# A 256-token, three-layer fp32 network: the third layer's two 16-column gate tiles as one tile with 48 stationary weight columns

## What is computed

```python
def rmsnorm_2(x, w):
    xf = x.astype(jnp.float32)
    xf = xf * lax.rsqrt(jnp.mean(xf * xf, axis=-1, keepdims=True) + EPS)
    return (xf * w.astype(jnp.float32)).astype(x.dtype)
...
    h = rmsnorm_2(x, ln1_w)
    proj = h @ w_in
    z, xbc, dt_raw, q, k, v, f_raw = jnp.split(proj, split_at, axis=-1)
...
    dt = jax.nn.softplus(dt_raw.astype(jnp.float32) + dt_bias.astype(jnp.float32))
...
    log_f = jax.nn.log_sigmoid(f_raw.astype(jnp.float32) + fox_f_bias.astype(jnp.float32))
```

## Time and profile before

| | us |
|---|---|
| median of three runs | 2963.93 (2962.32 to 2968.41) |
| the profiled execution | 2967.45 |
| its span | 2965.5 |
| TensorE matmul busy | 2497.8 (84%) |
| TensorE weight load busy | 1786.3 (60%) |
| VectorE busy | 1626.1 (55%) |
| ScalarE busy | 949.8 (32%) |
| mean granted TensorE clock | 0.97 of 2.4 GHz |

### The profile page before, as it was taken

One profiled execution on the slowest core, in us unless ns is written; L12 is line 12 of the kernel. 1 busy time (PEld: TensorE's weight loads), 2 busy tenths in 40 slices (PEclk: granted clock), 3 DMA queues, 4 the chain that ended last, 5 costly groups with the idle time before them and its releaser, 6 DMA issues.

```text
span 2965.5 us, 31159 instructions
## 1 busy us (share of the span) xinstructions
PE 2497.8 (84%) x12386; PEld 1786.3 (60%) x12386; DVE 1626.1 (55%) x2261; ACT 949.8 (32%) x1555; POOL 694.8 (23%) x751
## 2 busy tenths in 40 slices
PE   7999888999999999999899387777777677777776
PEld 6997877899898799789689332222222232222222
DVE  4757494544445544346556976656555444444444
ACT  4557455533775443343554110000010001000001
POOL 6003150000000000440000243333334343333331
PEclk9999999999999999899899699999999999999999
DMA  6644304555444535244255699999999999999997
GB/s 195 206 143 142 114 1 154 173 185 182 151 151 143 184 122 193 73 133 152 71 185 171 246 404 422 421 422 421 421 422 422 421 421 422 422 421 422 421 422 318
DMA packets 200416, 779.53 MB, mean 263 GB/s; under 512 B 16564, under 2 KB 20880, under 8 KB 134096
## 3 DMA queue, kind: packets, MB, share of 16 engines
q0 software_dynamic: 74400, 537.15, 43.8%
q1 hardware_dynamic: 125872, 240.40, 24.4%
HBM read 775.40 MB, written 2.10 MB: 262 GB/s over the span
## 4 chain that ended last, share of the span: by engine, by line
DMA 34%; PE 27%; DVE 5%; issue 1%; ACT 1%; POOL 0%; DVEq 0%; ACTq 0%; POOLq 0%
DMA VROW<-in_peer_v_dram,WORK 33%; PE bank L1720 26%; DMA UROW<-in_peer_u_dram,WORK 1%; DVE WL L1089 1%; DVE BIG L1680 1%; DVE WORK L1385 0%; DVE BIG L1386 0%; DVE WORK L1388 0%; DVE WORK L1387 0%; PE bank L1774 0%; DVE WORK L1384 0%; PE bank L1817 0%; DVE BIG L1395 0%; DVE WORK L1397 0%; DVE BIG L1393 0%
## 5 line engine op out<-in xcount | busy, mean ns | idle before, releaser
L1720 PE MATMUL bank<-VROW,WORK 128*128 128x512 f32 x2024 | 926.8, 603 | 368.2 <-DMA VROW<-in_peer_v_dram,WORK 301.2
L1720 PEld LDWEIGHTS bank<-VROW,WORK 128*128 128x128 f32 x2024 | 367.3, 190 | 927.0 <-issue 745.7
L1680 DVE CUSTOM_DVE_ANT_0 BIG<-UROW,bank 128x2048 f32<-128x2048 f32 x256 | 585.5, 2288 | 562.7 <-DMA UROW<-in_peer_u_dram,WORK 548.5
L1089 DVE TENSOR_TENSOR WL<-RAW,WH 128x1024 fp32r<-128x1024 f32 (+2 forms) x464 | 544.4, 1182 | 544.2 <-ACT WH L594 542.9
L594 ACT ACTIVATE WH<-RAW 128x1024 fp32r<-128x1024 f32 (+2 forms) x464 | 465.9, 1020 | 480.6 <-PE bank L1720 480.1
L1720 PE MATMUL bank<-HH,WH 128*128 128x256 f32 x2112 | 604.0, 286 | 8.0 <-issue 4.8
L1720 PE MATMUL bank<-HL,WH 128*128 128x256 f32 x2112 | 598.7, 283 | 0.0
L1720 PE MATMUL bank<-HH,WL 128*128 128x256 f32 x2112 | 598.5, 283 | 0.0
L1720 PEld LDWEIGHTS bank<-HH,WH 128*128 128x128 f32 x2112 | 406.2, 192 | 14.3 <-issue 12.2
L1720 PEld LDWEIGHTS bank<-HL,WH 128*128 128x128 f32 x2112 | 406.4, 192 | 0.0
L1720 PEld LDWEIGHTS bank<-HH,WL 128*128 128x128 f32 x2112 | 406.2, 192 | 0.0
(11 more groups left out here) (322 smaller groups left out, 1739.8 us busy)
## 6 DMA issues: line engine op xcount, KB each, us to landing
RAW<-in_w_in_odd_dram SPq DMA_DIRECT2D x64, 1024.0 KB, 5.0
RAW<-in_w_in_even_dram SPq DMA_DIRECT2D x48, 1024.0 KB, 5.0
RAW<-in_w_in_dram SPq DMA_DIRECT2D x44, 1024.0 KB, 4.9
RAW<-in_w_out_even_dram SPq DMA_DIRECT2D x16, 1024.0 KB, 5.0
RAW<-in_w_out_odd_dram SPq DMA_DIRECT2D x16, 1024.0 KB, 5.0
RAW<-in_w_out_dram SPq DMA_DIRECT2D x16, 1024.0 KB, 5.1
RAW<-in_peer_wq_dram SPq DMA_DIRECT2D x16, 1024.0 KB, 5.1
UROW<-in_peer_u_dram,WORK POOLq DMA_INDIRECT x256, 27.0
```

Of the source, the lines that this page charges most:

```text
L1089: dve.tensor_tensor(WL[:, sl:sl + 2, 0:w], raw[:, k0:k0 + 2, 0:w], WH[:, sl:sl + 2, 0:w].bitcast(F32), ALU.subtract).then_inc(s["wl_done"], 1)
L1680: dve.tensor_tensor_reduce(out=JUNK[:, n % 2, :], in0=UROW[:, b, :], in1=TT, op0=ALU.mult, op1=ALU.add, scale=1.0, scalar=0.0, accum_out=D ...
L1720: return pe.matmul(dst, lhsT, rhs, start=start, stop=stop, skip_group_check=True)
```

## The change

Tile 39 becomes one gate tile of 48 weight columns and tile 44 goes; all later tiles move up by one number (57 in all). Of the 48 columns, 32 are columns 2560 to 2591 (`dt_raw` and 16 of `q`, whose results are not used), 16 are `f_raw`. Each of the four pieces is loaded by two DMAs, each with a semaphore of its own, and ScalarE waits for both. The weights are the stationary side now, 256 tokens move: 6 matmuls per sub-step, 48 in all, into 48 partitions of one bank. ScalarE copies them to GATES_T unscaled; at place G_TURN TensorE turns them with two transposes into bank 5, and one place later ScalarE scales them into DTF with four small copies (`gates_out`). VectorE's F_GATE and S_GATE wait for those. S_CONV moves eight places up with the tiles that it follows; F_FIRST and S_GATE keep their place numbers.

```diff
@@ -77,9 +77,9 @@
         ("odd_out", [("w_out_odd", 0, 512, 4, "res", 0)]),
-        ("two_in", [("w_in_2", 2576, 512, 2, "eighth", 5), ("w_in_2", 5648, 16, 1, "gate", 1),
+        ("two_in", [("w_in_2", 2576, 512, 2, "eighth", 5), ("w_in_2", 2560, 48, 1, "gate", 0),
                     ("w_in_2", 3600, 512, 2, "chan", 7), ("w_in_2", 4624, 512, 2, "tok", 9),
-                    ("w_in_2", 2560, 16, 1, "gate", 0), ("w_in_2", 1024, 512, 3, "chan", 2),
+                    ("w_in_2", 1024, 512, 3, "chan", 2),
                     ("w_in_2", 0, 512, 2, "silu", 0)]),
...
@@ -124,10 +124,11 @@
 C_ACT_LAG, C_DVE_LAG = 2, 3
-F_GATE = 8 * TWO_TILE + 30
+G_TURN = 8 * TWO_TILE + 29
+F_GATE = 8 * TWO_TILE + 31
 F_FIRST = 8 * TWO_TILE + 47
 S_GATE = 8 * TWO_TILE + 70
-S_CONV = 8 * TWO_TILE + 86
+S_CONV = 8 * TWO_TILE + 78
 Q_TILE = last_tile("two_out") + 1
...
@@ -242,7 +243,7 @@
             const_in vec_in masks vec_t cols_set x_in lnf_in out_done eps_set act_chain dve_chain pool_chain
-            w_full0 w_full1 w_full2 w_full3 wh_done wl_done ws_used tile_free
+            w_full0 w_full1 w_full2 w_full3 w_gate0 w_gate1 w_gate2 w_gate3 g_t wh_done wl_done ws_used tile_free
             n_rstd n_sq n_sum n_x n_t n_xt n_h n_l r_diag r_row r_set t_scaled y_ready y_h y_l
...
@@ -294,6 +295,7 @@
                               two_slots(WORK[:, 2304:3072]))
+        GATES_T = WORK[0:48, 3200:3456]
         C_T, C_SP, C_W = (two_slots(WORK[:, 0:768]), two_slots(WORK[:, 768:1536]), two_slots(WORK[:, 1536:2304]))
@@ -338,7 +340,12 @@
                     c = bass.ds(r["c0"] + i * r["width"], r["width"])
-                    sp.dma_start(dst, src[:, 4 * j:4 * j + 4, c]).then_inc(s[f"w_full{j}"], 16)
+                    if r["kind"] == "gate":
+                        sp.dma_start(dst[:, :, 0:32], src[:, 4 * j:4 * j + 4, 2560:2592]).then_inc(s[f"w_gate{j}"], 16)
+                        sp.dma_start(dst[:, :, 32:48], src[:, 4 * j:4 * j + 4, 5648:5664]).then_inc(s[f"w_full{j}"], 16)
+                    else:
+                        sp.dma_start(dst, src[:, 4 * j:4 * j + 4, c]).then_inc(s[f"w_full{j}"], 16)
...
@@ -558,19 +565,29 @@
                 act.wait_ge(s["ws_used"], 8 * (t + 1))
+                if kind == "gate":
+                    act.activation(GATES_T, bank[2 * parity][0:48, 0:T], ACT.Copy).then_inc(s["tile_free"], 1)
+                    return
                 if kind != "plain":
...
                     rstd = SM[:, 20 + b:21 + b]
-                    if kind == "gate":
-                        ins = act.activation(DTF[:, r["dest"], b, :], ps[:, 0:16], ACT.Copy, scale=rstd)
-                    else:
-                        w = r["width"]
-                        ins = act.activation(BIG[:, r["dest"] + i, b * 512:b * 512 + w], ps[:, 0:w], ACT.Copy,
-                                             scale=rstd if kind == "tok" else 1.0)
+                    w = r["width"]
+                    ins = act.activation(BIG[:, r["dest"] + i, b * 512:b * 512 + w], ps[:, 0:w], ACT.Copy,
+                                         scale=rstd if kind == "tok" else 1.0)
                 ins.then_inc(s["tile_free"], 1)
+            def gates_out():
+                act.wait_ge(s["g_t"], 1)
+                act.wait_ge(s["n_rstd"], NORMED.index("two_in") + 1)
+                for b in range(2):
+                    for d in range(2):
+                        ins = act.activation(DTF[:, d, b, :], bank[5][:, 64 * b + 32 * d:64 * b + 32 * d + 16], ACT.Copy,
+                                             scale=SM[:, 20 + b:21 + b])
+                ins.then_inc(s["g_t"], 1)
...
@@ -585,6 +602,8 @@
                         act.wait_ge(s[f"w_full{sub // 2}"], 16 * (t + 1))
+                        if r["kind"] == "gate":
+                            act.wait_ge(s[f"w_gate{sub // 2}"], 16)
                     if r["base"] > 0 or not first or sub >= 4:
@@ -842,6 +861,8 @@
                     attend_step("f_", i, F_S, F_PROBS, F_PT, None)
+                if place == G_TURN + 1:
+                    gates_out()
                 if place == F_GATE + 2:
...
@@ -1466,7 +1487,7 @@
                 if place == F_GATE:
-                    dve.wait_ge(s["tile_free"], TWO_TILE + 3)
+                    dve.wait_ge(s["g_t"], 2)
                     link(dve.tensor_tensor(f_lf.rearrange(two, m=2), DTF[:, 1, :, :], per_head(F_FB), ALU.add))
...
@@ -1474,7 +1495,7 @@
                 if place == S_GATE:
-                    dve.wait_ge(s["tile_free"], TWO_TILE + 8)
+                    dve.wait_ge(s["g_t"], 2)
                     dve.tensor_tensor(s_dt.rearrange(two, m=2), DTF[:, 0, :, :], per_head(S_DTB), ALU.add)\
...
@@ -1486,7 +1507,7 @@
-                    dve.wait_ge(s["tile_free"], TWO_TILE + 9 + k // 4)
+                    dve.wait_ge(s["tile_free"], TWO_TILE + 8 + k // 4)
                     convolve(k)
@@ -1727,7 +1748,7 @@
                 w = r["width"]
-                toks = r["kind"] in ("tok", "res", "gate")
+                toks = r["kind"] in ("tok", "res")
                 for sub in range(8):
...
@@ -1751,6 +1772,11 @@
                                 ins = mm(dst, HH[:, kt, ms], WL[:, sl, 0:w], False, last)
+                        elif r["kind"] == "gate":
+                            dst = bank[2 * parity][0:w, 0:T]
+                            mm(dst, WH[:, sl, 0:w], HH[:, kt, :], kt == 0, False)
+                            mm(dst, WH[:, sl, 0:w], HL[:, kt, :], False, False)
+                            ins = mm(dst, WL[:, sl, 0:w], HH[:, kt, :], False, last)
                         else:
...
@@ -1971,6 +1997,12 @@
                     attend_step("a_", i, a_score, A_PROBS, A_PT, a_value, 0)
+                if place == G_TURN:
+                    pe.wait_ge(s["tile_free"], TWO_TILE + 3)
+                    for b in range(MT):
+                        ins = pe.transpose(bank[5][:, 64 * b:64 * b + 48], GATES_T[:, b * P:(b + 1) * P], ID[0:48, 0:48])
+                    ins.then_inc(s["g_t"], 1)
                 i = step_at(place, F_FIRST, 2, ATTEND_STEPS)
...
```

## The result

| | before | after |
|---|---|---|
| median of four runs, us | 2966.17 (2962.32 to 2968.49) | 2937.79 (2937.38 to 2939.42) |
| the profiled execution, us | 2967.45 | 2937.92 |
| its span, us | 2965.5 | 2936.2 |
| the stretch from the start of the first long TensorE piece to VectorE's bank copy at the phase's end, us | 1073.61 to 1401.06 = 327.45 | 1072.55 to 1371.59 = 299.04 |

After takes 0.9906 of the time of before (95% interval 0.9893 to 0.9918): 28.4 us less. The forecast was 28.1 us less, 2935.8 us, so the median came out 2.0 us above it. The difference was right to 0.3 us: a fourth run of before moved the median of before up by 2.2 us, from 2963.93.

The account below looks back on a forecast made before the run. TensorE alone was taken to bound the third layer's input projection. Removing 35.30 us, less 5.76 (new tile), 0.22 (transposes), 0.54 and 0.6 (waits), gives 28.2 us: 2935.8 us from the 2963.93 median, range 2929 to 2945.

Parts of the forecast that it names:

- The clock: In the two narrow gate tiles TensorE's granted clock falls to 0.50; removing them also recovers 13.8 us beyond the count.
- rival 2: The clock falls at about the same places anyway, so only the count goes: 14.4 us gained, 2949.5 us; chance 0.06.
- rival 1: The new gate tile, filling 48 of 128 weight columns, also loses the clock: 7.5 us given back, 2943.3 us; chance 0.09.
- The count: Both gate tiles: 192 matmuls at 0.112 us, 21.5 us, go; 48 at 0.120 us, 5.76 us, are added.
- The seam ahead of the next tile: The short gate tile releases weight slots late, so the next wide tile starts 0.54 us after the gate tile is issued.
- The turn: First wide tile: two transposes add 0.22 us, and ScalarE's wait for them stalls TensorE 0.6 us, bounds 0 and 1.5.
- VectorE beside convolutions and attention: Convolutions sharing eight places with the attention's tail: hidden, VectorE leaving with some 0.6 us of lead; bounds 0 and 2 us.
- rival 3: Feeding takes over: convolution overlap, turn and next load all at their upper bounds; 5.4 us back, 2941.2 us; chance 0.07.
- Loads: Gate load as eight DMAs, landing in 1.9 to 6.3 us, costed at nothing; the first due over 10 us after issue.
- The sum: All terms together: 35.30 - 5.76 - 0.22 - 0.54 - 0.6 = 28.2 us saved.
- four moved attention steps: Attention steps inside the second gate tile stay, moved beside wide tiles, at 3.23 us each: 12.92 of its 31.13 us.
- rival 4: Clock falls in the new tile and stays at 0.50 through three wide tiles: 75 us lost, 3010.7 us; chance 0.02.

Follow-up runs that it names:

- The added load: One more VectorE instruction of 0.41 us, a product nobody reads, ahead of each of the twelve convolutions in the changed kernel; 2938.83 us, beside 2937.74 for the changed kernel.

## Why the prediction was right

**The clock.** This was the term that could have failed. The prediction took 13.8 us of the removed time for half clock. The kernel before with 128 columns moving gives 14.1 in the stretch and 13.8 in the median, with no matmul fewer. The Trainium skill (TensorE: Matmul & The Clock Gate, Part 1) gives idle gaps of the engine as what loses the clock; for rival 2 that meant falls at the same places and a gain of 14.4 us. The runs show falls that no such gap explains: in the first gate tile and in the merged one with 48 moving columns TensorE and its weight loading were busy throughout when the clock fell. Rival 2 is out, since with 128 moving columns nothing fell at the same places, and so is rival 1, since neither 48 nor 16 stationary columns cost anything.

The second gate tile of the kernel before is less simple than the prediction has it. Its clock fell twice, and came back in between (windows of 2 us, and the transposes of the first two attention steps in it):

```profile
1236.00:1238.00 2.00, 2.00 (x11) 1.33 (x9) 0.50 (x1) 0.00 (x0) 0.50 (x1) 0.77 0.86 330
...
1252.00:1254.00 2.00, 2.00 (x17) 1.83 (x16) 1.30 (x1) 1.24 (x2) 2.00 (x3) 1.00 1.02 392
1254.00:1256.00 2.00, 2.00 (x8) 1.59 (x7) 0.00 (x0) 0.00 (x0) 0.09 (x1) 0.54 0.16 59
```

```profile
1231.36 0.49 PE L1817 MATMUL bank<-ID,WORK 128*128 128x128 f32 x3
...
1237.26 0.85 PE L1817 MATMUL bank<-ID,WORK 128*128 128x128 f32 x3
```

Both falls come inside an attention step, some 1.9 and 1.0 us behind the last narrow matmul, so the half clock slowed the attention's matmuls too: the same three transposes take 0.85 us instead of 0.49. With 128 columns moving in the gate tile the same steps ran at 1.00, so the narrow matmuls ahead of them are what the falls hang on; the size of the loss (13.8 us) is not touched by this.

**The count.** 192 matmuls at 0.112 us are 21.5 us, the new tile 5.64: 15.9 us saved. I had 5.76, taking the wide matmul's 0.120 for each; measured are 0.117. The estimate of 5.2 us that the prediction worked out from the Trainium skill (TensorE: Matmul & The Clock Gate, Back-to-back issue gap) was too low. A narrower stationary side saved nearly nothing: 0.117 us with 48 columns against 0.120 with 128, both with 256 moving. The Trainium skill (TensorE: Matmul & The Clock Gate, LDWEIGHTS) ties the time of a load to the stationary columns, 107 ns for 128. The traces agree: behind 128 stationary columns the pitch is 0.111 to 0.112 us whether 16, 48 or 128 columns move. That loading is what limits it there is read from these pitches; no run varied it by itself.

**The seam ahead of the next tile.** Predicted 0.54, measured 0.61 us, and 0.68 with the slower start of the matmuls behind it, released by VectorE's split as said. The start of the splits was read as 3.86 us into the tile; ScalarE's came at 3.78 (1111.40 - 1107.62), VectorE's 1.09 on, TensorE 1.38 after that: 6.25 of a predicted 6.30. The next tile came 0.05 us earlier than predicted, and the gap is still larger, since the gate tile itself was quicker by 0.12.

**The turn.** The wait was predicted at 0.6 us and measured at 0.27 (0.25 by moving it). The largest part is the time of the four copies: I took 0.21 each from the two in the earlier trace rows, 0.84 in all, and measured are 0.64. The transposes were predicted at 0.22 us and cost 0.44. The prediction took the pitch of transposes that run in a row. These two stand between wide matmuls: 0.21 us pass before the first of them instead of 0.12, and 0.23 behind the matmul that follows them. The two errors have opposite signs (0.82 predicted, 0.71 measured in all), which is luck.

**VectorE beside convolutions and attention.** Costed at nothing, with 0.6 us in hand; it was nothing, with 1.7 in hand. By the prediction's own terms (a lead of over 3 us, less 40.0 - 34.6 - 3.4 = 2.0) over 1 us was left, not 0.6. The added load shows that the work had been hidden and where that ends: rival 3 had a real mechanism there, and the change stopped short of it.

**Loads.** The gate load as eight DMAs was costed at nothing. Loads of the matrix from 1080 to 1130 us landed in 2.0 to 9.4 us (the median 2.9) against the earlier trace rows, and no split of the stretch was late by one. The first DMA of a piece is one of 64 KB, not of 32 as the prediction says; the second takes 0.51 us to issue, and no wait in the stretch is put down to it.

**The sum.** With the measured terms: 35.30 - 5.64 - 0.44 - 0.68 - 0.27 = 28.3, against 28.41 in the stretch. The 0.1 left is not assigned; the largest term with a guess in it is the 12.92 us for four moved attention steps. That the predicted sum, 28.2, lies so close is in part luck: it had the tile and the wait at the turn too high, the transposes and the seam too low.

Not tried: a moving side between 48 and 128 columns, and whether rival 4 (a clock that stays low through wide tiles) can occur anywhere. In the two kernels whose clock fell here it was back 3.9 and 2.7 us into the wide matmuls behind the first gate tile or the merged one.

## What to carry to other kernels

Before counting matmuls, read the granted clock in the windows of a narrow tile: at 16 or 48 moving columns it fell to half here though the engine was never idle, and simply moving 128 columns, most of them unused, gave back 13.8 us. Turning the product so that the long side moves and the few columns are stationary gives that and the smaller count at once; the transposes and the wait for the small copies behind them cost 0.7 us. A tile that gets shorter than the ring of buffers behind it starves the next one: work out when its slots come free, and give it slots of its own if the gap matters.

## What the runs showed of the hardware that was not expected

A matmul with 128 moving columns starts as often (0.111 us) as one with 16 (0.112 us) behind 128 stationary columns, so at full clock width on the moving side up to there was free. With 256 moving columns the stationary side hardly mattered: 0.120 us at 128 columns, 0.117 at 48, and 0.12 us less for the whole tile of 48 matmuls at 16. In the first gate tile TensorE's weight-load row was busy 2.00 of 2.00 us at half clock as at full clock (the window 1116 to 1118 us with 128 moving columns): busy time alone does not show the fall, but the count of loads does, 11 instead of 20. Two transposes set between wide matmuls cost 0.44 us, where three in a row take 0.33.
